# Up products of two transformer blocks: high-part and low-part matmuls taken tile by tile

## The chip, the cores and the metric

The kernel runs on one core of a Trainium2 chip. The metric is device time in microseconds (us), the median of several executions. The engines named below are TensorE (PE; PEld is its weight load), VectorE (DVE), ScalarE (ACT), GpSimd (POOL) and SyncE (SP), which issues the loads.

## The reference

Two blocks run one after the other over 256 tokens of width 2048 in float32. The first is one layer with four mixers and a feed-forward part; the second has two layers of latent attention with retention, each with a feed-forward part. The three feed-forward parts have the same shape (2048 to 8192 to 2048), and the change lies in the first product of each:

```python
        ff = jnp.square(jax.nn.relu(hn @ mlp_w1[l])) @ mlp_w2[l]          # first block, 1 layer
...
        x = x + jnp.square(jax.nn.relu(h @ w_up[l])) @ w_down[l]          # second block, 2 layers
```

## The kernel before

Each float32 weight is split into a high part and a low part that TensorE takes in its faster float32 form: ACT casts a loaded panel to `whi` (line 1592), and DVE subtracts, `wlo = raw - whi` (line 2295). The activations are split in the same way: `xT[:, k, :]` holds 256 columns of high part and 256 of low part. A product is then high weight by both halves of `xT` (a matmul of 512 columns, line 682, here called wide) plus low weight by the high half alone (256 columns, line 688, here called narrow), all into the same bank of PSUM.

An up stage makes 8192 output columns as 16 groups of 512. A group is four units, `u` = 0 to 3; a unit takes one loaded panel (four k-tiles of 128 rows by four column tiles `j` of 128), so 16 wide and 16 narrow matmuls. There are three up stages: 3 x 16 x 4 = 192 units. `whi` and `wlo` have two buffers each, used in turn by the units (`u % 2`). Semaphores order the work:

- `hi` and `lo` say that ACT's cast and DVE's subtraction of a unit's panel are done. TensorE waits for `hi` at the unit's head and for `lo` in `need_panel`. Each engine takes its instructions in program order, and DVE's subtraction waits for `hi`.
- `pan` rises at a unit's last matmul. ACT's cast for a unit waits until the unit two before it is done, since it writes the same buffer.
- `tile` and `pan` say in the last unit (`u` = 3) that a column tile is complete. ACT copies its low half out (line 1651), which raises `uph`; DVE adds the high half (line 2345), squares the positive part (line 2347) and raises `upd`. ACT and DVE take these four evictions behind the cast and the subtraction for unit 0 of the next group, and ahead of those for its unit 1.
- `xt` says that pieces of `xT` are ready. In the first up stage (`chunk` set) the first group starts while `xT` is still being made: TensorE transposes the remaining pieces of `x` between units (`chunk(u + 2)`, line 625), ACT scales them to the high part (line 1612), DVE makes the low part (line 2313). In the other two stages `xT` is half ready at the start, and the rest is transposed after unit 0 (`between`).

Stages follow one another without a common barrier; after each up stage come the down products (line 1167).

Of the kernel before, what the change touches and what calls it, by code (L numbers as in the profile page):

```python
# [27 lines left out]
P = 128  # L28
D = 2048
KD = D // P  # L30
CHUNKS = D // 512
SEQ = 256
# [213 lines left out]
def build(nc, A, out, place, n_const):  # L246
    with ExitStack() as ctx:
        def sb(name, shape, dtype=F32):
            return ctx.enter_context(nc.sbuf_tensor(name, shape, dtype))
# [3 lines left out]
        whi = sb("whi", [P, 2, 2048], F32R)  # L253
        wlo = sb("wlo", [P, 2, 2048], F32R)
# [3 lines left out]
        xT = xT1[:, :, :, :].rearrange("p k s t -> p (k s t)")[:, 0:KD * 2 * SEQ].rearrange(  # L258
            "p (k n) -> p k n", k=KD)
# [163 lines left out]
        sig = {n: ctx.enter_context(nc.semaphore(n)) for n in names}  # L423
        block = ctx.enter_context(nc.Block())

        def psum(bank, n=512, rows=P, at=0):
            return ps[0:rows, bank, at:at + n]
# [164 lines left out]
        def _(pe):  # L592
            st = Steps()
            mm, tr = pe.matmul, pe.transpose
# [23 lines left out]
            def need_panel(Q, u):  # L618
                pe.wait_ge(sig["lo"], 4 * Q + u + 1)
# [39 lines left out]
            def up(norm_at, even=0, between=None, chunk=None):  # L659


                odd = 4 - even
                at = st.stage("up")
                Q = at["quad"]

                def group(Q, g4, bank, wait_tiles, first=False, between=None):
                    for u in range(4):

                        pe.wait_ge(sig["hi"], 4 * Q + u + 1)
                        for j in range(4):  # L670
                            if first and not chunk:

                                pe.wait_ge(sig["xt"], norm_at["xt"] + max(2 * u + 2, j + 1))
                            if u == 0 and wait_tiles:

                                pe.wait_ge(sig["upd"], g4 + j - 7)
                            for kk in range(4):
                                k = 4 * u + kk
                                c = kk * 512 + j * P
                                if first and chunk and j == 0 and kk % 2 == 0:  # L680
                                    pe.wait_ge(sig["xt"], norm_at["xt"] + k // 2 + 1)
                                mm(psum(bank + j), whi[:, u % 2, c:c + P], xT[:, k, :], start=k == 0, stop=False)  # L682
                        need_panel(Q, u)
                        for j in range(4):
                            for kk in range(4):
                                k = 4 * u + kk
                                c = kk * 512 + j * P
                                last = mm(psum(bank + j, SEQ), wlo[:, u % 2, c:c + P], xT[:, k, 0:SEQ],  # L688
                                          start=False, stop=k == KD - 1)
                            if u == 3 and j < 3:  # L690
                                last.then_inc(sig["tile"], 1)
                        last.then_inc(sig["pan"], 1)
                        if u == 0 and between:
                            between()
                        if first and chunk and u < 2:
                            chunk(u + 2)

                group(Q, at["upd"], even, False, first=True, between=between)
                group(Q + 1, at["upd"] + 4, odd, False)
                with pe.Fori(1, 8) as i:  # L700
                    group(Q + 2 * i, at["upd"] + 8 * i, even, True)
                    group(Q + 2 * i + 1, at["upd"] + 8 * i + 4, odd, True)
                return at

            norm_at = st.stage("first_norm")
# [20 lines left out]
            for j in range(2):  # L726
                last = tr(psum(2, P, at=P * j), xm[:, P * j:P * j + P], ident)
# [9 lines left out]
            Q = at["quad"]  # L737
# [283 lines left out]
            Q = at["quad"]  # L1021
# [2450 lines left out]
```

## Time and profile before

| what | value |
|---|---|
| median of 3 runs | 3261.62 us (3261.45 to 3261.71) |
| profiled execution: time | 3262.3 us |
| profiled execution: span, first to last instruction | 3260.5 us |
| instructions | 45588 |
| granted TensorE clock, mean | 0.999 |

The page of the profile gives busy time by engine, then groups of instructions with their mean duration. A matmul's duration in the records is its latency; consecutive matmuls overlap, so their pace is read from one start to the next in the timeline. A timeline row such as "487.00 3.82 PE L682 ... x16" says that 16 matmuls of line 682 began at 487.00 us, the last of them ending 3.82 us later.

### The profile page before, as it was taken

The page shows a single profiled execution, that of the slowest core. Times are in us where ns is not written, and L with a number is a line of the kernel's source. Part 1 is how long each engine was busy: PE and PEld are TensorE (multiplying, and loading weights), DVE is VectorE, ACT ScalarE, POOL GpSimd, SP SyncE. Part 2 cuts the span into 40 slices and gives each one's busy share as a digit, 9 for nine tenths or more (in the row PEclk, how much of TensorE's full clock was granted, in tenths as well). Part 3 has the DMA queues.
Part 4 walks back from the last instruction along what each step waited for, and adds up shares of the span by engine and source line. Part 5 has one row for each costly group of instructions (what it writes and reads, how often), then busy time and mean ns, then how long its engine had stood idle before and what let it go on. Part 6 is the DMA issues. An engine that isn't in the chain of part 4 may idle for free.

```text
span 3260.5 us, 45588 instructions
## 1 busy us (share of the span) xinstructions
PE 3236.0 (99%) x17237; PEld 2792.2 (86%) x17237; DVE 2180.9 (67%) x2584; ACT 1568.1 (48%) x1830; POOL 267.8 (8%) x211
## 2 busy tenths in 40 slices
PE   8999999999999999999999999999999999999999
PEld 8999888888888888888888888888888888888887
DVE  7888665557865656565555688875656555568887
ACT  5336453445554544544434455554454534445555
POOL 6422000000000024000000000001400000000000
PEclk9999999999999999999999999999999999999999
DMA  7544565555665555455555566655545565556564
GB/s 211 163 134 155 194 200 187 193 185 189 206 194 193 165 178 181 142 181 181 187 190 190 186 200 200 200 178 176 183 150 175 192 193 189 184 189 198 195 204 155
DMA packets 249327, 598.65 MB, mean 184 GB/s; under 512 B 22296, under 2 KB 64248, under 8 KB 248184
## 3 DMA queue, kind: packets, MB, share of 16 engines
q1 hardware_dynamic: 248056, 591.17, 56.2%
q0 software_dynamic: 768, 5.24, 0.4%
q8 instruction: 83, 1.36, 0.2%
q10 hardware_dynamic: 384, 0.58, 0.0%
q14 instruction: 36, 0.29, 0.0%
HBM read 594.86 MB, written 2.10 MB: 183 GB/s over the span
## 4 chain that ended last, share of the span: by engine, by line
PE 96%; DVE 2%; ACT 1%; DVEq 0%; DMA 0%; issue 0%; SPq 0%; ACTq 0%
PE ps L1167 26%; PE ps L682 21%; PE ps L1422 18%; PE ps L688 11%; PE ps L1119 5%; PE ps L1070 3%; PE ps L756 2%; PE ps L764 2%; PE ps L757 2%; PE ps L1479 1%; PE ps L625 1%; PE ps L1474 1%; DVE wlo L2295 1%; PE ps L1316 0%; PE ps L1314 0%; DMA x<-in_x 0%
## 5 line engine op out<-in xcount | busy, mean ns | idle before, releaser
L2295 DVE TENSOR_TENSOR wlo<-raw,whi 128x2048 fp32r<-128x2048 f32 (+1 forms) x425 | 971.2, 2286 | 571.7 <-ACT whi L1592 571.2
L1592 ACT CAST whi<-raw 128x2048 fp32r<-128x2048 f32 x425 | 805.6, 1896 | 495.5 <-PE ps L688 426.9
L682 PE MATMUL ps<-xT,whi 128*128 128x512 f32 x3072 | 733.5, 391 | 1.4 <-DVE xT L2313 1.1
L682 PEld LDWEIGHTS ps<-xT,whi 128*128 128x128 f32 x3072 | 564.6, 188 | 111.5 <-issue 1.3
L1167 PE MATMUL ps<-whi,stage 128*128 128x512 f32 x2480 | 593.3, 389 | 0.0
L1167 PEld LDWEIGHTS ps<-whi,stage 128*128 128x128 f32 x2480 | 465.2, 188 | 96.3
L1422 PE MATMUL ps<-whi,xT 128*128 128x512 f32 (+1 forms) x1792 | 444.2, 388 | 1.1 <-DVE wlo L2998 0.9
L688 PEld LDWEIGHTS ps<-xT,wlo 128*128 128x128 f32 x3072 | 393.9, 191 | 15.0
L688 PE MATMUL ps<-xT,wlo 128*128 128x256 f32 x3072 | 398.5, 283 | 0.0
L2998 DVE TENSOR_TENSOR wlo<-raw,whi 128x2048 fp32r<-128x2048 f32 (+3 forms) x126 | 275.8, 2189 | 171.1 <-ACT whi L2058 171.0
L1422 PEld LDWEIGHTS ps<-whi,xT 128*128 128x128 f32 x1792 | 326.2, 188 | 63.4 <-issue 1.7
L1986 ACT CAST stage<-big 128x256 fp32r (+3 forms) x384 | 133.3, 394 | 457.9 <-PE ps L1167 368.7
L2058 ACT CAST whi<-raw 128x2048 fp32r<-128x2048 f32 (+3 forms) x125 | 224.2, 1793 | 253.3 <-PE ps L1422 227.4
L1167 PE MATMUL ps<-wlo,stage 128*128 128x512 f32 x1240 | 312.3, 389 | 0.0
L1167 PEld LDWEIGHTS ps<-wlo,stage 128*128 128x128 f32 x1240 | 232.5, 188 | 49.4 <-DVE wlo L2295 1.2
L1422 PE MATMUL ps<-wlo,xT 128*128 128x512 f32 (+1 forms) x896 | 235.9, 388 | 0.0
L1422 PEld LDWEIGHTS ps<-wlo,xT 128*128 128x128 f32 x896 | 164.4, 188 | 31.5
L2872 DVE TENSOR_TENSOR stage<-big,stage 128x256 fp32r<-128x256 f32 (+1 forms) x384 | 145.0, 414 | 57.5 <-ACT stage L1986 57.2
L1651 ACT COPY up_lo<-ps 128x256 f32<-128x256 f32 x192 | 71.6, 373 | 170.9 <-PE ps L688 106.3
L756 PE MATMUL ps<-xT,whi 128*128 128x272 f32 x560 | 146.3, 295 | 0.9 <-issue 0.9
L757 PE MATMUL ps<-xT,whi 128*128 128x272 f32 x560 | 142.8, 288 | 0.0
L756 PEld LDWEIGHTS ps<-xT,whi 128*128 128x128 f32 x560 | 105.8, 189 | 5.9 <-issue 5.6
(495 smaller groups left out, 3009.2 us busy)
## 6 DMA issues: line engine op xcount, KB each, us to landing
raw<-in_mlp_w SPq DMA_DIRECT2D x128, 1024.0 KB, 5.1
raw<-in_w_up SPq DMA_DIRECT2D x128, 1024.0 KB, 5.2
raw<-in_w_down SPq DMA_DIRECT2D x128, 1024.0 KB, 5.3
raw<-in_w_in SPq DMA_DIRECT2D x100, 1024.0 KB, 5.1
raw<-in_w_o SPq DMA_DIRECT2D x32, 1024.0 KB, 5.3
raw<-in_w_out SPq DMA_DIRECT2D x16, 1024.0 KB, 5.1
raw<-in_w_in SPq DMA_DIRECT2D x16, 832.0 KB, 4.4
raw<-in_w_uq SPq DMA_DIRECT2D x8, 768.0 KB, 4.4
```

The source lines that it names most:

```text
L682: mm(psum(bank + j), whi[:, u % 2, c:c + P], xT[:, k, :], start=k == 0, stop=False)
L688: last = mm(psum(bank + j, SEQ), wlo[:, u % 2, c:c + P], xT[:, k, 0:SEQ], start=False, stop=k == KD - 1)
L756: mm(psum(j, L), hi, xT1[:, k, 0, :], start=k == 0, stop=False)
L757: mm(psum(j, L), hi, xT1[:, k, 1, :], start=False, stop=False)
L1119: return mm(psum(bank), x_, w, start=start, stop=stop)
L1167: return mm(psum(bank + 2 * r + n), x_of(kk, part, r), w[:, u % 2, c:c + 512], start=begin and kk == part == 0 and w is whi, stop=stop)
L1422: return mm(psum(bank + n_of * r + n, widths[n]), x_of(ks * i + kk, part, r), w[:, s, c:c + widths[n]], start=begin and kk == part == 0 an ...
L1592: act.copy(whi[:, u % 2, 0:width], raw[:, u, 0:width]).then_inc(sig["hi"], 1)
L2058: act.copy(whi[:, p % 2, 0:panel_width(p)], raw[:, p % 4, 0:panel_width(p)]).then_inc(sig["hi"], 1)
L2295: tt(wlo[:, u % 2, 0:width], raw[:, u, 0:width], whi[:, u % 2, 0:width].bitcast(F32), SUB).then_inc(sig["lo"], 1)
L2872: tt(stage[:, k, SEQ:SEQ + n], hT[:, bass.ds(k0 + kk, 1), 0:n].rearrange("p o n -> p (o n)"), stage[:, k, 0:n].bitcast(F32), SUB).then_inc ...
L2998: tt(wlo[:, p % 2, 0:w], raw[:, p % 4, 0:w], whi[:, p % 2, 0:w].bitcast(F32), SUB).then_inc(sig["lo"], 1)
```

## The change

Within a unit, before, the 16 wide matmuls came first, then one wait for `lo`, then the 16 narrow ones. Now the unit is taken by column tile: four wide matmuls of tile `j`, then its four narrow ones, for `j` = 0 to 3; the wait for `lo` stands after the first four wide ones. Matmuls, operands and banks are the same, and so is the number of waits and increments. The new line numbers are 681 (wide) and 685 (narrow).

```diff
                         pe.wait_ge(sig["hi"], 4 * Q + u + 1)
                         for j in range(4):
-                            if first and not chunk:
-
-                                pe.wait_ge(sig["xt"], norm_at["xt"] + max(2 * u + 2, j + 1))
-                            if u == 0 and wait_tiles:
-
-                                pe.wait_ge(sig["upd"], g4 + j - 7)
+                            ready(j)
                             for kk in range(4):
-                                k = 4 * u + kk
-                                c = kk * 512 + j * P
-                                if first and chunk and j == 0 and kk % 2 == 0:
-                                    pe.wait_ge(sig["xt"], norm_at["xt"] + k // 2 + 1)
-                                mm(psum(bank + j), whi[:, u % 2, c:c + P], xT[:, k, :], start=k == 0, stop=False)
-                        need_panel(Q, u)
-                        for j in range(4):
+                                high(j, kk)
+                            if j == 0:
+                                need_panel(Q, u)
                             for kk in range(4):
-                                k = 4 * u + kk
-                                c = kk * 512 + j * P
-                                last = mm(psum(bank + j, SEQ), wlo[:, u % 2, c:c + P], xT[:, k, 0:SEQ],
-                                          start=False, stop=k == KD - 1)
-                            if u == 3 and j < 3:
-                                last.then_inc(sig["tile"], 1)
+                                last = low(j, kk)
                         last.then_inc(sig["pan"], 1)
```

`ready`, `high` and `low` hold the removed lines unchanged (the waits for `xt` and `upd`, the wide matmul, the narrow matmul); in unit 3 the last narrow matmul of tile `j` raises `tile`, as before.

On TensorE, at the head of the first up stage (unit 0 of its first group), there stood before:

```order
L682 MATMUL ps<-xT,whi 128x512 [waits xt,hi]
L682 MATMUL ps<-xT,whi 128x512
L682 MATMUL ps<-xT,whi 128x512 [waits xt]
L682 MATMUL ps<-xT,whi 128x512 x13
L688 MATMUL ps<-xT,wlo 128x256 [waits lo]
L688 MATMUL ps<-xT,wlo 128x256 x15
L625 MATMUL ps<-cst,x 128x128 [waits xt,resid]
```

And there stands now:

```order
L681 MATMUL ps<-xT,whi 128x512 [waits xt,hi]
L681 MATMUL ps<-xT,whi 128x512
L681 MATMUL ps<-xT,whi 128x512 [waits xt]
L681 MATMUL ps<-xT,whi 128x512
L685 MATMUL ps<-xT,wlo 128x256 [waits lo]
L685 MATMUL ps<-xT,wlo 128x256 x3
L681 MATMUL ps<-xT,whi 128x512 x4
L685 MATMUL ps<-xT,wlo 128x256 x4
```

The wait for `lo` has moved from behind 16 wide matmuls to behind four. The last two rows repeat for the other tiles, and then the transposes of line 625 follow as before.

On TensorE, in the loop over the later groups, unit 1 stood before as

```order
L682 MATMUL ps<-xT,whi 128x512 [waits hi]
L682 MATMUL ps<-xT,whi 128x512 x15
L688 MATMUL ps<-xT,wlo 128x256 [waits lo]
L688 MATMUL ps<-xT,wlo 128x256 x15
L669 REGISTER_ALU
```

and stands now as

```order
L681 MATMUL ps<-xT,whi 128x512 [waits hi]
L681 MATMUL ps<-xT,whi 128x512 x3
L685 MATMUL ps<-xT,wlo 128x256 [waits lo]
L685 MATMUL ps<-xT,wlo 128x256 x3
L681 MATMUL ps<-xT,whi 128x512 x4
```

(narrow and wide then go on in fours). A unit had one step from wide to narrow and one back to the next unit's wide ones; it now has four of each. DVE, ACT, POOL and SP keep their order.

## Rows read from the trace of the kernel before

**Rows 1.** The page: busy time and the group of the wide up matmuls.

```profile
PE 3236.0 (99%) x17237; PEld 2792.2 (86%) x17237; DVE 2180.9 (67%) x2584; ACT 1568.1 (48%) x1830; POOL 267.8 (8%) x211
...
L682 PE MATMUL ps<-xT,whi 128*128 128x512 f32 x3072 | 733.5, 391 | 1.4 <-DVE xT L2313 1.1
```

**Rows 2.** Timeline of a steady unit: start us, us, engine, line, operation, operands, count.

```profile
501.59 2.29 DVE L2295 TENSOR_TENSOR wlo<-raw,whi 128x2048 fp32r<-128x2048 f32 x1 [0.41 <-ACT whi L1592]
...
503.70 3.82 PE L682 MATMUL ps<-xT,whi 128*128 128x512 f32 x16
...
507.36 2.08 PE L688 MATMUL ps<-xT,wlo 128*128 128x256 f32 x16
...
509.27 3.82 PE L682 MATMUL ps<-xT,whi 128*128 128x512 f32 x16
```

**Rows 3.** Timeline cut inside that unit: its fifth wide, then its fifth narrow matmul.

```profile
504.63 0.85 PE L682 MATMUL ps<-xT,whi 128*128 128x512 f32 x3
...
507.83 0.64 PE L688 MATMUL ps<-xT,wlo 128*128 128x256 f32 x4
```

**Rows 4.** One width only: 72 of 512 (chain), then eight of 256 (timeline).

```profile
781.49 16.32 PE ps L1167 x72
...
1198.62 1.12 PE L1479 MATMUL ps<-stage,whi 128*128 128x256 f32 x8
1199.58 0.64 PE L1474 MATMUL ps<-whi,stage 128*128 128x256 f32 x4
```

**Rows 5.** Timeline of the latent kv products: four of 512, then eight of 256.

```profile
1215.41 1.09 PE L1474 MATMUL ps<-whi,ckv 128*128 128x512 f32 x4
1216.35 1.11 PE L1479 MATMUL ps<-ckv,whi 128*128 128x256 f32 x8
1217.29 0.63 PE L1474 MATMUL ps<-wlo,ckv 128*128 128x512 f32 x2
```

**Rows 6.** Timeline of 512 and 320 columns in strict turn (eight pairs).

```profile
1119.65 3.20 PE L1422 MATMUL ps<-whi,xT 128*128 128x512 f32 x16
1122.69 0.54 PE L1422 MATMUL ps<-wlo,xT 128*128 128x512 f32 x2
```

**Rows 7.** Timeline of a matmul that waited for a low part.

```profile
1477.96 2.28 DVE L2998 TENSOR_TENSOR wlo<-raw,whi 128x2048 fp32r<-128x2048 f32 x1
...
1480.38 0.69 PE L1422 MATMUL ps<-whi,xT 128*128 128x512 f32 x2 [0.45 <-DVE wlo L2998]
```

**Rows 8.** Timeline of the first six units of the first up stage.

```profile
406.40 4.16 PE L682 MATMUL ps<-xT,whi 128*128 128x512 f32 x16 [1.11 <-DVE xT L2313]
...
406.95 2.28 DVE L2295 TENSOR_TENSOR wlo<-raw,whi 128x2048 fp32r<-128x2048 f32 x1
...
412.31 1.03 PE L625 MATMUL ps<-cst,x 128*128 128x128 f32 x8
...
419.40 1.57 ACT L1612 ACTIVATE xT<-ps,cols 128x256 fp32r<-128x256 f32 x4 [3.08 <-PE ps L625]
...
424.69 2.29 DVE L2295 TENSOR_TENSOR wlo<-raw,whi 128x2048 fp32r<-128x2048 f32 x1 [2.76 <-ACT whi L1592]
...
425.22 3.82 PE L682 MATMUL ps<-xT,whi 128*128 128x512 f32 x16
...
430.53 2.28 DVE L2295 TENSOR_TENSOR wlo<-raw,whi 128x2048 fp32r<-128x2048 f32 x1
...
430.78 3.59 PE L682 MATMUL ps<-xT,whi 128*128 128x512 f32 x15
...
436.78 4.49 DVE L2295 TENSOR_TENSOR wlo<-raw,whi 128x2048 fp32r<-128x2048 f32 x2 [0.63 <-ACT whi L1592]
...
436.80 3.92 PE L682 MATMUL ps<-xT,whi 128*128 128x512 f32 x16 [0.29 <-ACT whi L1592]
```

**Rows 9.** Timeline: the tightest low part of the second up stage.

```profile
1513.20 2.29 DVE L2295 TENSOR_TENSOR wlo<-raw,whi 128x2048 fp32r<-128x2048 f32 x1 [0.64 <-ACT whi L1592]
...
1515.52 3.82 PE L682 MATMUL ps<-xT,whi 128*128 128x512 f32 x16
```

More of the change, by code:

```diff
@@ L667, in group, with ready @@
                     for u in range(4):
-                        pe.wait_ge(sig["hi"], 4 * Q + u + 1)
-                        for j in range(4):
+                        def ready(j):
                             if first and not chunk:
@@ L676, in group, with high, low @@
                                 pe.wait_ge(sig["upd"], g4 + j - 7)
-                            for kk in range(4):
-                                k = 4 * u + kk
-                                c = kk * 512 + j * P
-                                if first and chunk and j == 0 and kk % 2 == 0:
-                                    pe.wait_ge(sig["xt"], norm_at["xt"] + k // 2 + 1)
-                                mm(psum(bank + j), whi[:, u % 2, c:c + P], xT[:, k, :], start=k == 0, stop=False)
-                        need_panel(Q, u)
-                        for j in range(4):
-                            for kk in range(4):
-                                k = 4 * u + kk
-                                c = kk * 512 + j * P
-                                last = mm(psum(bank + j, SEQ), wlo[:, u % 2, c:c + P], xT[:, k, 0:SEQ],
-                                          start=False, stop=k == KD - 1)
-                            if u == 3 and j < 3:
-                                last.then_inc(sig["tile"], 1)
+                        def high(j, kk):
+                            k, c = 4 * u + kk, kk * 512 + j * P
+                            if first and chunk and j == 0 and kk % 2 == 0:
+                                pe.wait_ge(sig["xt"], norm_at["xt"] + k // 2 + 1)
+                            mm(psum(bank + j), whi[:, u % 2, c:c + P], xT[:, k, :], start=k == 0, stop=False)
+                        def low(j, kk):
+                            k, c = 4 * u + kk, kk * 512 + j * P
+                            last = mm(psum(bank + j, SEQ), wlo[:, u % 2, c:c + P], xT[:, k, 0:SEQ],
+                                      start=False, stop=k == KD - 1)
+                            if u == 3 and j < 3 and kk == 3:
+                                last.then_inc(sig["tile"], 1)
+                            return last
+                        pe.wait_ge(sig["hi"], 4 * Q + u + 1)
+                        for j in range(4):
+                            ready(j)
+                            for kk in range(4):
+                                high(j, kk)
+                            if j == 0:
+                                need_panel(Q, u)
+                            for kk in range(4):
+                                last = low(j, kk)
                         last.then_inc(sig["pan"], 1)
```

## Prediction, made before the changed kernel was run

> **What bounds the kernel now.** I read the page first. TensorE is busy for 3236.0 us of the 3260.5 us span, 99% [rows 1]. The wide up matmuls waited 1.4 us in all over 3072 instructions [rows 1]. So in the up stages nothing stands between TensorE and the end: what makes its stream longer makes the kernel longer by as much, and a wait can hardly be taken away because there is none to speak of. The change can act in two ways only: through the pace of the stream when wide and narrow matmuls alternate more often, and through the wait for `lo`, which now comes earlier in the unit.
>
> I then read the timeline of a steady unit. Its 16 wide matmuls begin at 503.70 and its 16 narrow ones at 507.36, and the next unit's at 509.27 [rows 2]: 3.66 us + 1.91 us = 5.57 us. Next I looked for the pace of each width by itself. 72 matmuls of 512 columns in a row take 16.32 us, 0.2267 us each, and eight of 256 take 0.96 us, 0.120 us each [rows 4]. Pure streams would need 16 x 0.2267 + 16 x 0.120 = 5.547 us for a unit. The real unit is 0.02 us longer, and it holds one round trip from wide to narrow and back. A cut through the unit shows where this lies: the first four wide matmuls take 0.93 us (503.70 to 504.63) where four at the pure pace take 0.907, and the first four narrow ones take 0.47 us (507.36 to 507.83) where the pure pace gives 0.48 [rows 2, 3]. The other twelve of each run go at about the pure pace. A step to narrow gives a little back, and a step to wide costs a little more.
>
> **The change, part by part.** Nothing is added or removed in number: 16 wide and 16 narrow matmuls a unit, the same banks, waits and increments. Moved are three quarters of both kinds, the `lo` wait, and the `tile` increments.
>
> *Steps between widths.* A unit now makes four round trips where it made one. Every run of four is then a "first four" as in rows 3. For wide ones I take +0.023 us over the pure pace (0.93 - 0.907). For narrow ones I take -0.007 us; the whole narrow run confirms it, 1.91 us against 16 x 0.120 = 1.92 [rows 2, 4]. A round trip costs +0.016 us, and four cost 0.064 us; the unit before has 0.02 us of it already, so a unit grows by about 0.045 us, to 5.61 us. There are 3 x 16 x 4 = 192 units: 192 x 0.045 = **+8.6 us**. The trace has no run of four wide and four narrow, so I bound it from both sides. Four of 512 and eight of 256 in the latent kv products take 1.88 us (1215.41 to 1217.29), against 4 x 0.2267 + 8 x 0.120 = 1.867 [rows 4, 5]: +0.013 us a round trip, or +0.03 us a unit, 6 us in all. The low bound is strict turn-taking: eight pairs of 512 and 320 columns take 3.04 us, 0.380 us a pair [rows 6]; with 320 columns interpolated between the two pure paces to 0.147 us the pair should take 0.373, so a round trip costs 0.007 us, a unit grows by 4 x 0.007 - 0.02 = 0.007 us, and all units by 1.3 us. The high bound leaves out the gain of the narrow runs: 4 x 0.023 - 0.02 = 0.072 us, 13.8 us in all. I take 0.045 because it comes from the same matmuls, widths and engine neighbours; the kv products have longer narrow runs.
>
> The Trainium skill ("TensorE: Matmul & The Clock Gate", section "Back-to-back issue gap") gives the isolated gap of a matmul at full clock as its columns over 2.4 GHz plus about 2.5 ns, whatever stands beside it. By its figures a unit would take some 5.2 us in either order and these steps would cost nothing; the trace disagrees on both paces (226.7 and 120 ns against about 216 and 109) and shows the first four of a run off the pace of the rest.
>
> *The wait for `lo` in steady units.* The tightest is unit 1 of a group, whose cast and subtraction stand behind the four evictions: the subtraction ends at 501.59 + 2.29 = 503.88 [rows 2]. A low part that is waited for releases TensorE about 0.14 us after its end (1477.96 + 2.28 = 1480.24, matmul at 1480.38) [rows 7], so it is usable at 504.02. The first narrow matmul will be due at 504.63, where the fifth wide one stood [rows 3]. The margin was over 3 us and is now 0.6 us, and still no wait. It should even grow, since `tile` for tiles 0 to 2 rises earlier in unit 3 and the evictions can start as soon as DVE has done its subtraction. I put this at nothing; if the cover were gone, each 0.1 us of lateness would cost 0.1 us in each of some 45 groups, 4.5 us. In the second up stage the tightest low part ends at 1513.20 + 2.29 = 1515.49, usable at 1515.63, and is due at 1515.52 + 0.93 = 1516.45 [rows 9]: no wait; the third up stage runs the same code with the same order of work, and I cost it alike.
>
> *The wait for `lo` at the head of the first up stage.* Here DVE and ACT are still making `xT` and low parts come late.
> Unit 0 starts at 406.40. Its wide run is 0.34 us longer than a steady one (4.16 against 3.82), so the first four end at 406.40 + 0.93 + 0.34 = 407.67. Its low part ends at 406.95 + 2.28 = 409.23, usable at 409.37 [rows 2, 7, 8]. TensorE waits 1.70 us where it waited for nothing, and resumes slower: after a wait the second matmul of a pair started about 0.30 us behind the first (0.69 - 0.39, with 0.39 us the duration of one) instead of 0.227, 0.07 us more [rows 1, 7]. Together 1.77 us.
> The transposes behind unit 0 (412.31) and unit 1, ACT's scaling behind them (419.40, released by TensorE) and the casts behind that shift along [rows 8]. After two units the shift is 1.77 + 2 x 0.045 = 1.86 us. Unit 3 starts at 425.22, and its low part ends at 426.98, usable 1.90 us into the unit, due 0.93 us into it [rows 8]: 0.97 + 0.07 - 0.05 (TensorE is one more grown unit behind) = 0.99 us.
> Unit 0 of the next group starts at 430.78 + 1.77 + 0.99 + 0.18 = 433.72 and wants its low part at 434.65; this ended at 432.81, and now at 432.95 + 1.86 = 434.81 [rows 8]: 0.16 + 0.07 = 0.23 us.
> Unit 1 started at 436.80, after a wait for its cast: without it, at 430.78 + 5.57 = 436.35, and its wide run was 0.10 us longer (3.92 against 3.82). This 0.55 us is absorbed. It now starts at 436.35 + 2.94 + 0.05 + 0.23 = 439.57 and wants its low part at 440.50; this comes at 436.78 + 2.25 + 0.14 + 1.86 = 441.03 [rows 8]: 0.53 + 0.07 = 0.60 us. From unit 2 on the pattern is the steady one.
> Sum: 1.77 + 0.99 + 0.23 + 0.60 - 0.55 = **+3.0 us**. Behind a waiting narrow matmul stand all later matmuls of TensorE, and ACT's casts through `pan`, so none of it is regained. If only the first wait comes true, it is 1.77 - 0.55 = 1.2 us.
>
> *Earlier `tile`.* An earlier last eviction could only shorten a wait at the head of the down products, and these run at the pure pace [rows 4]. Nothing.
>
> Sum: 8.6 + 3.0 = 11.6 us. The profiled execution took 3262.3 us for a span of 3260.5; the median of the runs is 3261.62, 0.7 us below it, and I add to the median: **3273.2 us**, 0.36% slower.
>
> **The rivals.** A measurement here can tell about 0.2%, 6.5 us (3255.1 to 3268.1).
> *Steps cost next to nothing.* If a step is priced as in rows 6, the sum is 1.3 + 3.0 = 4.3 us, 3265.9 us; if nothing, the unit falls to 5.547 us, -3.8 + 3.0 = -0.8 us, 3260.8 us. For it: in strict turns the excess is only 0.007 us. Against it: every wide run after narrow ones read here starts slow [rows 3, 5]. 0.13. The rule cited above would land here.
> *Faster: the slow start belongs to long narrow runs.* If the excess of wide runs comes only after many narrow matmuls and four are too few, while each narrow run still gains its 0.007 us, a unit takes 5.547 - 4 x 0.007 = 5.519 us, 0.048 us less than before: -9.2 + 3.0 = -6.2 us, 3255.4 us. It turns the sign once a round trip costs less than about +0.001 us (the point at which -0.016 us a unit pays the 3.0 us). Against it: the kv rows have a positive net after eight narrow ones [rows 5]. 0.03.
> *Steady low parts come late after all.* The 0.6 us margin is gone if evictions or casts move by that much, and then each group waits: 0.2 us late with 0.07 us refill is 45 x 0.27 = 12 us more, 3285 us. It speaks for it that the margin shrinks by 2.7 us; against it that the work ahead of this subtraction moves earlier. 0.05.
> The forecast, steps as in rows 3 and waits in the first up stage alone, has 0.79.
>
> **How the numbers follow.** The forecast's own bounds are 1.3 + 3.0 and 13.8 + 3.0 us, 3265.9 to 3278.4 us. I give 3265 to 3279, which leaves out the last two rivals and the lower half of the first, some 0.15. Faster by over 0.2% is the second rival, 0.03; within it is the first rival, 0.13; slower is the rest, 0.84.
>
> **What would show it.** Steady unit: starts of consecutive units 5.61 us apart, wide runs of four about 0.93 us apart from the narrow ones, which take 0.47. Head of the first up stage: a wait of about 1.7 us on DVE's subtraction before the first narrow matmul, one near 1 us in unit 3, small ones in the next two units; no wait for the low part elsewhere. ACT's first eviction copy should start earlier against unit 3's head than before. Wrong would be a unit of 5.55 us, or idle time before the narrow matmuls in the loop.

## The result and the profile after

The changed kernel takes 3273.85 us (median of 6 runs, 3273.35 to 3276.45) against 3261.53 us of the kernel before on the same chips: 12.3 us more, ratio 1.0039, 95% interval 1.0028 to 1.0051. The forecast was 3273.2 us. Its profiled execution has a span of 3271.6 us; the first wide up matmul came 0.92 us earlier in it than in the profile of before (405.48 against 406.40 [rows 8]), a difference ahead of the change, so the spans differ by 11.1 us. From the first wide up matmul of the first stage to the last narrow one of the third, where all of the change lies, it is 11.8 us more: 2518.8 against 2507.0 us.

The page shows a longer span, TensorE still busy for 99% of it, and a new wait: the narrow matmuls now waited 2.6 us for DVE's subtraction, where [rows 1] had the wide ones waiting 1.4 us in all. (The busy times of the two groups are larger because each now counts the overlap at its many ends; the counts are what they were, and the wide ones' mean duration is 394 ns against 391 [rows 1].)

```profile
span 3271.6 us, 45588 instructions
...
PE 3244.6 (99%) x17237; PEld 2787.9 (85%) x17237; DVE 2177.7 (67%) x2584; ACT 1562.2 (48%) x1830; POOL 267.4 (8%) x211
...
L681 PE MATMUL ps<-xT,whi 128*128 128x512 f32 x3072 | 839.1, 394 | 1.1 <-DVE xT L2321 1.1
...
L685 PE MATMUL ps<-xT,wlo 128*128 128x256 f32 x3072 | 489.1, 281 | 2.6 <-DVE wlo L2303 2.6
```

The timeline of a steady group, to be read beside [rows 2, 3]. The rows are PE runs, with ACT's cast and DVE's subtraction for the group's unit 1:

```profile
500.92 1.09 PE L681 MATMUL ps<-xT,whi 128*128 128x512 f32 x4
...
501.89 1.91 ACT L1600 CAST whi<-raw 128x2048 fp32r<-128x2048 f32 x1
...
503.83 2.29 DVE L2303 TENSOR_TENSOR wlo<-raw,whi 128x2048 fp32r<-128x2048 f32 x1 [0.39 <-ACT whi L1600]
...
506.53 1.09 PE L681 MATMUL ps<-xT,whi 128*128 128x512 f32 x4
...
507.46 0.64 PE L685 MATMUL ps<-xT,wlo 128*128 128x256 f32 x4
...
507.94 1.09 PE L681 MATMUL ps<-xT,whi 128*128 128x512 f32 x4
...
508.87 0.63 PE L685 MATMUL ps<-xT,wlo 128*128 128x256 f32 x4
...
512.15 1.09 PE L681 MATMUL ps<-xT,whi 128*128 128x512 f32 x4
```

Unit 1 goes from 506.53 to 512.15, 5.62 us, where a unit took 5.57. Its four wide matmuls take 0.93 us (506.53 to 507.46), its four narrow ones 0.48 (507.46 to 507.94), the next wide ones 0.93 again. The low part of this unit ends at 503.83 + 2.29 = 506.12, ahead of the unit's own head, and is due at 507.46: a margin of 1.2 us with the 0.14 us that the prediction took for the release, where [rows 2, 3] gave 0.6 with the old eviction times. The earlier `tile` moved the evictions and with them the cast, as the prediction had it: DVE's first addition began 1.27 us ahead of unit 0's head, where it was 0.76 us before, and the cast 4.64 us ahead of unit 1's head, where it was 4.06 us.

The head of the first up stage, to be read beside [rows 8]:

```profile
405.48 1.43 PE L681 MATMUL ps<-xT,whi 128*128 128x512 f32 x4 [1.11 <-DVE xT L2321]
...
406.03 2.28 DVE L2303 TENSOR_TENSOR wlo<-raw,whi 128x2048 fp32r<-128x2048 f32 x1
...
408.37 0.74 PE L685 MATMUL ps<-xT,wlo 128*128 128x256 f32 x4 [1.46 <-DVE wlo L2303]
...
408.94 1.09 PE L681 MATMUL ps<-xT,whi 128*128 128x512 f32 x4
...
425.55 2.29 DVE L2303 TENSOR_TENSOR wlo<-raw,whi 128x2048 fp32r<-128x2048 f32 x1 [2.75 <-ACT whi L1600]
...
426.11 1.09 PE L681 MATMUL ps<-xT,whi 128*128 128x512 f32 x4
...
427.90 0.74 PE L685 MATMUL ps<-xT,wlo 128*128 128x256 f32 x4 [0.70 <-DVE wlo L2303]
...
432.69 1.09 PE L681 MATMUL ps<-xT,whi 128*128 128x512 f32 x4
...
433.73 0.74 PE L685 MATMUL ps<-xT,wlo 128*128 128x256 f32 x4
...
437.65 2.29 DVE L2303 TENSOR_TENSOR wlo<-raw,whi 128x2048 fp32r<-128x2048 f32 x1 [0.64 <-ACT whi L1600]
...
438.50 1.09 PE L681 MATMUL ps<-xT,whi 128*128 128x512 f32 x4
...
440.00 0.74 PE L685 MATMUL ps<-xT,wlo 128*128 128x256 f32 x4 [0.40 <-DVE wlo L2303]
```

And where its sixth unit ends (the next unit's first wide matmul):

```profile
444.79 1.09 PE L681 MATMUL ps<-xT,whi 128*128 128x512 f32 x4
```

The same place in the kernel before:

```profile
442.47 3.82 PE L682 MATMUL ps<-xT,whi 128*128 128x512 f32 x16
```

Unit 0: four wide matmuls from 405.48, and the narrow ones only at 408.37, 2.89 us in, though they were due 1.27 us in: 1.62 us late. They then take 0.57 us (408.37 to 408.94) instead of 0.47, 0.10 us of slower restart. Unit 3 (426.11): narrow ones 1.79 us in, 0.86 us late. Unit 0 of the next group (432.69): 1.04 us in, 0.11 us late. Unit 1 (438.50): 1.50 us in, 0.57 us late. Six units and what lies between took 444.79 - 405.48 = 39.31 us; before, 442.47 - 406.40 = 36.07 [rows 8]. Of the 3.24 us between them six times the longer unit (5.613 instead of 5.567 us) makes 0.28, which leaves 2.96 us for late low parts, less the wait for a cast that is gone. From the end of the subtraction to the matmul that it releases it is 0.06 us here, not 0.14: 406.03 + 2.28 = 408.31 and 408.37, 425.55 + 2.29 = 427.84 and 427.90, 437.65 + 2.29 = 439.94 and 440.00.

### The profile page after: what moved, and what is told of

Same layout as the page of the kernel before. It is cut to its first block, busy times and chain, and to the rows that moved or that the text cites. A ratio compares the mean times of both kernels' runs of the same rounds, so it can differ in the third digit from the quotient of the medians.

```text
span 3271.6 us, 45588 instructions
## 1 busy us (share of the span) xinstructions
PE 3244.6 (99%) x17237; PEld 2787.9 (85%) x17237; DVE 2177.7 (67%) x2584; ACT 1562.2 (48%) x1830; POOL 267.4 (8%) x211
## 4 chain that ended last, share of the span: by engine, by line
PE 95%; DVE 3%; ACT 1%; DVEq 0%; DMA 0%; issue 0%; SPq 0%; ACTq 0%
PE ps L1175 26%; PE ps L681 21%; PE ps L1430 18%; PE ps L685 11%; PE ps L1127 5%; PE ps L1078 3%; PE ps L764 2%; PE ps L772 2%; PE ps L765 2%; PE ps L1487 1%; PE ps L625 1%; DVE wlo L2303 1%; PE ps L1482 1%; PE ps L1324 0%; PE ps L1322 0%; DMA x<-in_x 0%
## 5 line engine op out<-in xcount | busy, mean ns | idle before, releaser
L681 PE MATMUL ps<-xT,whi 128*128 128x512 f32 x3072 | 839.1, 394 | 1.1 <-DVE xT L2321 1.1
L681 PEld LDWEIGHTS ps<-xT,whi 128*128 128x128 f32 x3072 | 525.0, 189 | 72.2 <-issue 1.3
L685 PEld LDWEIGHTS ps<-xT,wlo 128*128 128x128 f32 x3072 | 471.1, 189 | 69.3 <-DVE wlo L2303 4.3
L685 PE MATMUL ps<-xT,wlo 128*128 128x256 f32 x3072 | 489.1, 281 | 2.6 <-DVE wlo L2303 2.6
L764 PEld LDWEIGHTS ps<-xT,whi 128*128 128x128 f32 x560 | 105.2, 188 | 6.3 <-issue 6.0
```

Of the source, the lines that this page charges most:

```text
L764: mm(psum(j, L), hi, xT1[:, k, 0, :], start=k == 0, stop=False)
```

## The experiments

All were compared with the kernel before on the same chip; their edits are shown against the changed kernel. The order inside a unit is written as a list of places (tile `j`, k-tile `kk`) that is cut into runs; `early`, a new argument of `group`, is set for the first two groups of a stage, `chunk` in the first stage:

```diff
                         pe.wait_ge(sig["hi"], 4 * Q + u + 1)
-                        for j in range(4):
-                            ready(j)
-                            for kk in range(4):
-                                high(j, kk)
-                            if j == 0:
-                                need_panel(Q, u)
-                            for kk in range(4):
-                                last = low(j, kk)
+                        run = 4 if not (chunk and early) else 16
+                        places = [(j, kk) for j in range(4) for kk in range(4)]
+                        for at_ in range(0, 16, run):
+                            for j, kk in places[at_:at_ + run]:
+                                if kk == 0:
+                                    ready(j)
+                                high(j, kk)
+                            if at_ == 0:
+                                need_panel(Q, u)
+                            for j, kk in places[at_:at_ + run]:
+                                last = low(j, kk)
```

| kernel | units in the new order | median us | same chip, before | ratio (95%) |
|---|---|---|---|---|
| fours, head as before | 184, runs of 4 | 3270.16 | 3261.56 | 1.0026 (1.0016 to 1.0036) |
| head only | 8, runs of 4 | 3266.29 | 3261.56 | 1.0015 (1.0006 to 1.0024) |
| eights | 184, runs of 8 | 3265.51 | 3261.56 | 1.0012 (1.0003 to 1.0021) |
| twos | 184, runs of 2 | 3262.67 | 3261.72 | 1.0003 (0.9994 to 1.0013) |
| ones | 184, runs of 1 | 3271.8 | 3261.56 | 1.0035 (1.0022 to 1.0048) |
| wide low parts, sixteens | 0 | 3583.95 | 3261.72 | 1.0988 (1.0971 to 1.1005) |
| wide low parts, fours | 184, runs of 4 | 3584.43 | 3261.72 | 1.0989 (1.0972 to 1.1006) |
| narrow first in unit 2 | 44 | 3261.41 | 3261.72 | 1.0000 (0.9991 to 1.0009) |

**Fours, with the head of the first stage as before** (the diff above).

> The first two groups of the first up stage keep the order of before (16 wide, 16 narrow); all 184 other units take fours, as in the change. If the 12.3 us are the sum of steps between widths (0.046 us a unit) and late low parts in those two groups (3.0 us), this takes 3261.5 + 184 x 0.046 = 3270.0 us, and TensorE waits for no low part in an up stage. If the late low parts cost nothing in the end, because what they delay is regained, it takes 3273.5 us, as the change does without the eight units' steps.

It took 3270.16 us. The table of waits by engine has no entry in which a narrow up matmul (line 685 here) waits; only the two waits of the wide ones (line 681) that the kernel before also had are left. Columns: waiting, waited for, us in total, times, longest:

```profile
PE ps L681 <- DVE xT L2324: 1.1, 1, 1.1
...
PE ps L681 <- ACT whi L1603: 0.3, 1, 0.3
```

**Head only**: `run = 4 if (chunk and early) else 16`.

> The reverse: only the first two groups of the first up stage take fours, the rest keeps the order of before. By the sum of both causes: 3261.5 + 3.0 + 8 x 0.046 = 3264.9 us, with the waits near 1.5, 0.7 and 0.4 us on the low part that the changed kernel shows, and steady units of 5.567 us. If the head only looks late and is regained: 3261.9 us.

It took 3266.29 us, 4.7 us more, 1.4 us above the sum that was expected; the interval (2.0 to 7.8 us more) holds the 3.4 expected and leaves out 0.3. Its executions range from 3264.83 to 3268.88 us. The two with a mean granted clock of 1.000 took 3264.83 and 3265.13 us, 3.3 and 3.6 us more than the median before, and the four with 0.998 are the four longest, 3267.40 us and more; that the clock makes the spread is not tested. In its trace the waits are those of the changed kernel:

```profile
PE ps L685 <- DVE wlo L2306: 2.6, 3, 1.5
```

The two halves, 8.6 and 4.7 us, make 13.3 us beside the 12.3 us of the whole change. The traces add up more closely: from the first to the last up matmul the first half is 8.41 us longer than the kernel before (2515.44 against 2507.02), the second 3.35 us (2510.37), together 11.76, and the whole change 11.82. Both causes are there.

**Eights**: `run = 8 if not (chunk and early) else 16`.

> Runs of eight (two column tiles wide, the same two narrow), the first two groups as before: two round trips between widths a unit. If every round trip costs the same (0.046/3 = 0.015 us more than the one that was there), a unit takes 5.582 us and the kernel 3261.5 + 184 x 0.015 = 3264.4 us. If the slow start lasts over five wide matmuls as in the units of before, two round trips cost 0.02 us each: 5.587 us, 3265.2 us. If the loss were the interleaving as such and not the number of steps, it would stay near 5.613 us, 3270.0 us.

It took 3265.51 us, 3.95 us more, the second of the three cases. PE's timeline inside steady units, two runs of each width a unit:

```profile
603.78 2.00 PE L681 MATMUL ps<-xT,whi 128*128 128x512 f32 x8
605.62 1.12 PE L685 MATMUL ps<-xT,wlo 128*128 128x256 f32 x8
606.58 2.00 PE L681 MATMUL ps<-xT,whi 128*128 128x512 f32 x8
608.42 1.12 PE L685 MATMUL ps<-xT,wlo 128*128 128x256 f32 x8
609.37 1.32 PE L681 MATMUL ps<-xT,whi 128*128 128x512 f32 x5
```

Two round trips take 5.59 us (603.78 to 609.37) where pure paces [rows 4] give 5.547: 0.02 us each, as with sixteens. A wide run of eight takes 1.84 us against 8 x 0.2267 = 1.81.

Why eights cost per round trip what sixteens do can be read from the starts of single matmuls in the trace of the kernel before. In every steady unit the first five wide matmuls start 233, 236, 228, 232 and 231 ns before the next one, and the others 227; the first two narrow ones 113 and 119 ns, and the others 120. The slow start lasts five matmuls, so a run of eight holds all of it and a run of four only about 0.023 us of its 0.027.

**Ones**: `run = 1 if not (chunk and early) else 16`.

> Strict turns: one wide, one narrow, 16 round trips a unit, the first two groups as before. If a round trip costs 0.0165 us however short its runs are, a unit takes 5.547 + 16 x 0.0165 = 5.811 us and the kernel 3261.5 + 184 x 0.244 = 3306 us. If it costs 0.007 us as in the strict turns of 512 and 320 columns, a unit takes 5.659 us and the kernel 3278.5 us. Below 5.613 us a unit, strict turns would be cheaper than fours, and the slow start would need runs.

Strict turns, ten pairs from 603.90 to 607.43:

```profile
603.90 0.40 PE L681 MATMUL ps<-xT,whi 128*128 128x512 f32 x1
604.13 0.28 PE L685 MATMUL ps<-xT,wlo 128*128 128x256 f32 x1
604.25 0.40 PE L681 MATMUL ps<-xT,whi 128*128 128x512 f32 x1
...
607.43 0.40 PE L681 MATMUL ps<-xT,whi 128*128 128x512 f32 x1
```

A pair takes 3.53 / 10 = 0.353 us against 0.2267 + 0.120 = 0.3467: 0.0063 us a round trip, close to the 0.007 of [rows 6]. Over all steady units of this trace a unit takes 5.653 us, 0.0067 us a round trip. The profiled execution took 3277.04 us, close to 3278.5. Its five executions fall on two levels, though: two at 3277.0 and 3277.8, three at 3271.5 to 3271.8. The trace belongs to the upper one. If the whole difference lies in the units, one took about 5.567 + (3271.5 - 3261.6) / 184 = 5.62 us at the lower; no trace of that level was kept, and why a program has two levels stays open.

**Twos**: `run = 2 if not (chunk and early) else 16`.

> Runs of two, eight round trips a unit, first two groups as before. Round trips cost 0.020, 0.020, 0.0165 and 0.0064 us with runs of 16, 8, 4 and 1. If the cost follows how many matmuls of a wide run stand in its slow start, two have about 0.007 + 0.009 us and give back 0.007 us: 8 x 0.010 = 0.08 us over 5.547, 5.627 us a unit, 3272.6 us. If runs of two cost as much as fours, 0.0165 us: 5.679 us, 3282 us; if as little as ones, 0.0064 us: 5.598 us, 3267 us.

All three expected values were wrong: 3262.67 us, 1 us above the kernel before, which the measurement doesn't tell from it. PE's timeline (eight runs of each width to a unit, of which the first and the last are shown):

```profile
604.07 0.63 PE L681 MATMUL ps<-xT,whi 128*128 128x512 f32 x2
604.53 0.40 PE L685 MATMUL ps<-xT,wlo 128*128 128x256 f32 x2
604.76 0.63 PE L681 MATMUL ps<-xT,whi 128*128 128x512 f32 x2
605.23 0.39 PE L685 MATMUL ps<-xT,wlo 128*128 128x256 f32 x2
...
609.64 0.62 PE L681 MATMUL ps<-xT,whi 128*128 128x512 f32 x2
```

Eight round trips take 5.57 us (604.07 to 609.64), 0.696 us each against a pure 0.693. Two wide matmuls take 0.46 to 0.47 us (0.453 at the pure pace), so they do start slow; but the two narrow ones behind them take 0.23 (0.24 at the pure pace) and give most of it back. The slow start of a wide run is not a fixed fee for a step. The first expected value, 0.010 us a round trip, came from cutting the run of before after two matmuls, as the prediction had cut it after four; for pairs that way of pricing was wrong by a factor of three.

**Wide low parts.** The low weight multiplies both halves of the activations, so that every matmul has 512 columns and writes the whole bank; once in the order of before, once in fours:

```diff
-                            last = mm(psum(bank + j, SEQ), wlo[:, u % 2, c:c + P], xT[:, k, 0:SEQ],
+                            last = mm(psum(bank + j), wlo[:, u % 2, c:c + P], xT[:, k, :],
                                       start=False, stop=k == KD - 1)
```

> The low-part matmuls take 512 columns instead of 256 (low weight by both halves of the activations, a product that the kernel before leaves out), in the order of before. No width changes in a unit, while the weight buffer does. If the slow start comes from the step of width, a unit takes 32 x 0.2267 = 7.253 us and the kernel about 3261.5 + 192 x 1.686 = 3585 us. If it comes from the switch of weight buffer, units are 0.02 us longer.

> The same wide low-part matmuls (low weight by both halves), taken in fours as in the change, the first two groups of the first up stage in the order of before. Step of width as the cause: 7.253 us a unit again, the same time as with sixteens within 0.1%. Switch of weight buffer or of bank as the cause: 0.046 us a unit more, 8.5 us in all.

They took 3583.95 and 3584.43 us, 0.5 us apart, not 8.5. The timelines of sixteens and of fours, at one place of the first stage:

```profile
603.33 3.79 PE L681 MATMUL ps<-xT,whi 128*128 128x512 f32 x16
606.96 3.79 PE L685 MATMUL ps<-xT,wlo 128*128 128x512 f32 x16
610.59 3.79 PE L681 MATMUL ps<-xT,whi 128*128 128x512 f32 x16
```

```profile
604.48 1.07 PE L685 MATMUL ps<-xT,wlo 128*128 128x512 f32 x4
605.39 1.07 PE L681 MATMUL ps<-xT,whi 128*128 128x512 f32 x4
606.29 1.07 PE L685 MATMUL ps<-xT,wlo 128*128 128x512 f32 x4
...
609.92 0.84 PE L685 MATMUL ps<-xT,wlo 128*128 128x512 f32 x3
```

Both run at the pure pace: 32 matmuls from 603.33 to 610.59, 7.26 us; 24 from 604.48 to 609.92, 5.44 us, 0.2267 each. Changing from `whi` to `wlo` or from one bank to the next costs nothing here: the steady units of both traces take 7.253 us, the pure pace. The slow start comes with the change of width, and with what goes with it here, that a narrow matmul reads half of the activations and writes half of the bank; no run separates these.

**Narrow first in unit 2.** The order of before with one round trip less in 44 groups:

```diff
+                        low_first = u == 2 and not first and not (chunk and early)
+                        if low_first:
+                            need_panel(Q, u)
+                        for kind in (low, high) if low_first else (high, low):
+                            if kind is low and not low_first:
                                 need_panel(Q, u)
...
+                            for j in range(4):
+                                if kind is high:
+                                    ready(j)
+                                for kk in range(4):
+                                    last = kind(j, kk)
```

> The order of before, but in unit 2 of 44 groups (all but each stage's first and the first stage's second) the narrow matmuls come first and the wide ones after, so that narrow follows narrow and wide follows wide across the unit borders: one round trip less for a group. If a round trip costs 0.02 us and the low part is there at the unit's head, the kernel takes 3261.5 - 44 x 0.02 = 3260.6 us, which the units in the trace can show and the time can't. If the low part is late at the unit's head, TensorE waits on DVE there, and it is slower: 0.1 us late is 4.4 us.

```profile
551.32 4.00 PE L685 MATMUL ps<-xT,wlo 128*128 128x256 f32 x32
555.16 7.44 PE L681 MATMUL ps<-xT,whi 128*128 128x512 f32 x32
...
573.57 4.00 PE L685 MATMUL ps<-xT,wlo 128*128 128x256 f32 x32
```

32 narrow matmuls stand in a row from 551.32, 32 wide ones from 555.16, and a group takes 573.57 - 551.32 = 22.25 us instead of 4 x 5.567 = 22.27. The median, 3261.41 us, is 0.3 us under the kernel before, which the measurement doesn't tell from nothing. In one place the low part came late, in the second group of the third stage, where ACT also makes a sum of squares: DVE's subtraction ended at 2587.49 + 2.29 = 2589.78, when the seventeenth of the 32 narrow matmuls was due at about 2587.77 + 16 x 0.120 = 2589.69:

```profile
2587.49 2.29 DVE L2306 TENSOR_TENSOR wlo<-raw,whi 128x2048 fp32r<-128x2048 f32 x1 [3.05 <-ACT whi L1603]
...
2587.77 4.30 PE L685 MATMUL ps<-xT,wlo 128*128 128x256 f32 x32
...
2591.91 0.40 PE L681 MATMUL ps<-xT,whi 128*128 128x512 f32 x1
```

With 0.14 us for the release, as in [rows 7], that is 0.23 us late. Those 32 took 4.14 us (to 2591.91) instead of 3.84: 0.3 us lost, a third of the 0.9 us to be had. No version here is faster than the kernel before by more than the measurement can tell.

## Why the prediction was right

- **TensorE's stream is the bound, and nothing is regained.** Held: each part of the change that lengthened the stream, or made it wait, was there in the time, and in the traces the parts, 8.41 and 3.35 us, make up the 11.82 us of the whole.
- **Steps between widths, +8.6 us.** A unit grew from 5.567 to 5.613 us, as forecast, and the kernel with only this part was 8.6 us slower. That a step of width is the cause was argued before; the kernels without a change of width show it. What does not hold is the price as a constant for each round trip, which the bounds rested on: it is 0.020 us with runs of 16 and of 8, 0.017 with runs of 4, 0.003 with runs of 2 and 0.007 with runs of 1. The forecast took four matmuls from the head of each long run [rows 2, 3] and supposed that a run of four would go like them. It did (+0.0225 and -0.006 us where +0.023 and -0.007 were taken), but nothing known beforehand made that sure: the same step failed for twos. Its accuracy was in part luck. The low bound from strict turns was right for strict turns alone.
- **Late low parts at the head of the first stage, +3.0 us.** Late by 1.62, 0.86, 0.11 and 0.57 us where 1.70, 0.92, 0.16 and 0.53 were forecast, and the refill 0.10 us where 0.07 was taken; 2.96 us net. Two terms were mis-sized and partly cancelled: the release took 0.06 us in each of the waits listed above, not the 0.14 us of [rows 7], and the refill was longer. In [rows 7], and in the one late low part of the kernel with narrow first, 0.14 us came where TensorE had a second wait, on `hi`, at the same matmul; in the changed kernel the wait for `lo` stands alone. The kernel with this part alone was 4.7 us slower in the median and 3.35 us in the trace, where 3.0 and the eight units' steps (0.37) make 3.4.
- **No late low part in steady units.** Held, and the margin grew, from the evictions that start earlier. The two later stages had no wait either: the three waits of the list are those of 1.46, 0.70 and 0.40 us at the head of the first stage (the fourth late low part, 0.11 us late, is too short for it), and in the trace the units of the later stages take 5.61 us from a stage's third on.
- **The rivals.** Steps that cost nothing: excluded for runs of four. Faster, with the slow start bound to long narrow runs: wrong for fours, though twos show that short runs do pay back nearly all. Steady low parts late: not seen.

The formula of the Trainium skill ("TensorE: Matmul & The Clock Gate", "Back-to-back issue gap") for the isolated gap at full clock, columns over 2.4 GHz plus 2.5 ns, has nothing in it but a matmul's own columns. Where widths don't change, the traces too show one gap for each width, 226.7 and 120.0 ns, each 13.3 ns above the columns over 2.4 GHz. Where widths change, the neighbours matter, and there the measurement decides. The same section of the Trainium skill says that in a stream of weight loads and matmuls both set the spacing, and gives about 131 ns for 512 columns there; no run here shows that pace.

## What to carry to other kernels

Before interleaving two kinds of matmul, find a place in the trace where each runs alone, cut the present order just behind a switch, and price the new order from the starts, since durations and busy times don't show the pace. And list for every operand the moment when it is first needed in the new order against the moment when it is ready, at the stage's head as well as in the steady part: here 188 of 192 units had a margin to spare and four did not, which cost a quarter of the loss. The stream of the bounding engine had next to no waits left, and no order tried here, with more switches or with fewer, was measurably faster. A price read from the head of a long run need not hold for a short run: it did for four matmuls and not for two.

## What the runs showed of the hardware

- A wide matmul run that follows narrow matmuls starts slow, also when loads, banks and clock stay the same (mean granted clock 0.998 to 1.000 in every execution); with equal widths in fours or sixteens the pace is 0.2267 us throughout.
- The slow start lasts five wide matmuls and costs 27 ns in all; a narrow run gives back 7.5 ns in its first two. The cost of a round trip is not monotonic in the run length. Mean excess over the pure paces (226.7 and 120 ns a matmul), from start to start over the steady units of each trace:

| wide and narrow in runs of | wide run, ns | narrow run, ns | round trip, ns |
|---|---|---|---|
| 16 | +27.5 | -7.5 | 20.0 |
| 8 | +27.5 | -7.5 | 20.0 |
| 4 | +22.5 | -5.8 | 16.7 |
| 2 | +12.9 | -9.6 | 3.3 |
| 1 | +9.7 | -3.0 | 6.7 |

- Why pairs come out nearly free is not explained by any run here. The row of ones is from a trace of the upper of its two levels.
- Strict turns gave two levels of time, 3271.5 and 3277 us, in executions of the same program.
- A subtraction on DVE released the waiting matmul 0.06 us after its end where that was the only wait, and 0.14 us after it where a second wait stood at the same matmul. Four narrow matmuls after such a wait took 0.57 us instead of 0.47.
